# A hybrid decoder layer on one core: where ScalarE's two exponentials stand among its copies in the sparse attention

## The chip, the cores and the metric

The kernel runs on one NeuronCore of a Trainium2 chip. Its engines take their instructions in order, each from a queue of its own: TensorE (PE, with its weight loads as PEld), VectorE (DVE), ScalarE (ACT), GpSimd (POOL), and SyncE (SP), which here only issues transfers. They wait for each other through semaphores. The metric is the device time of one execution in microseconds (us).

## The reference, and what of it matters here

The layer is `LayerNorm(ALPHA * x + TokenMixer(x))` followed by `LayerNorm(ALPHA * x + MoE(x))` for 1024 tokens of width 1024. The token mixer projects x to 7308 columns and splits them among a convolution, a sliding window attention, a retention, and a native sparse attention. The last has three parts: attention over compressed keys, over chosen blocks of keys, and over a window of 512 keys:

```
kcmp = compress(kc, pe_k, w1_k, w2_k)
...
p_cmp = masked_softmax(sc, cdist >= 0)
...
_, sel = lax.top_k(imp, min(NSA_TOPN, nslc))
...
o_win = banded_attention(qh, kw[:, None], vw[:, None], slopes, NSA_WINDOW)
...
o = gt[0] * o_cmp + gt[1] * o_slc + gt[2] * o_win
```

The kernel computes the part over chosen blocks as attention over all keys up to the query, with a penalty on the blocks that were not chosen.

## The kernel before

The mixers are the first stage of the program, up to about 971 us; then come the merge of the four branches, the output projection, and the experts. In the mixers one list, `SCHEDULE`, written by `schedule()`, sets the order. Each engine's program walks through the whole list and issues its own share of each item. So an item that moves in the list moves on each engine that does something for it, and only there.

The projection is cut into quarters (`('mm', q)`: 12 matmuls on TensorE, L537). Two quarters make a half, which ScalarE copies out of its PSUM bank (L744 for the merge gates, with a store on its own queue, L746). The attention works on pairs of heads. The sparse attention has 32 pairs, numbered 16 to 47: for each block n of 128 queries (0 to 7) and each pair of heads c one of kind `win`, with min(n+1, 5) blocks of keys, and one of kind `sel`, with n+1 blocks. `attention(NSA, ...)` writes one step for each pair. A step holds, in this order:

- `score` of the coming pair k+1: matmuls on TensorE (L707) into banks that `max` of the pair before must have read;
- `max` of both heads of pair k+1: VectorE adds the distance term (L1021), reduces (L1024), and writes the negated maximum `m_neg` (L1029);
- `norm` of both heads of pair k on VectorE (L1040, L1041, L1047), after their exponentials; for a `sel` pair a table (L1003) goes ahead;
- for pair k-1 its probabilities in groups of two blocks of keys. For each group: `fill`, which is four transposes on TensorE into bank 6 (L544) and a copy of the bank to `w_t` on ScalarE (L835), both 128x512, or 128x256 where a last group has one block; then, where their turn has come, quarters of the projection; then `pv`, the product with the values (L729, for the first group of a `win` pair also L724) of the group before, on TensorE. A finished block of queries is copied to `out_t` by ScalarE (`out`, L843) behind the product that completes it, and GpSimd stores it (L508);
- `exp` of both heads of pair k+1 on ScalarE (L855, with a second, short instruction that reads the sum).

Bank 6 is a single buffer, so transposes of a group wait for the copy of the group before:

```
B = bank[6]
if f:
    pe.wait_ge(fill_out, f)
```

ScalarE's exponential waits for VectorE:

```
act.wait_ge(max_done, u + 1)
```

And the first product of a new block of queries waits for the copy of the last one but itself:

```
if first and c == 0 and t:
    pe.wait_ge(tile_out, t)
```

Of the kernel before, what the change touches and what calls it, by code (L numbers as in the profile page):

```python
# [162 lines left out]
def schedule():  # L163

    items = [('xt', g) for g in range(8)] + [('mm', 0), ('mm', 1)] + [('xt', g) for g in range(8, 16)]
    state = dict(q=2, fill=0, pv=0)
    last = 4 * NCH

    def adv(n):
        for _ in range(n):
            if state['q'] < last:
                items.append(('mm', state['q']))
                state['q'] += 1

    def upto(c):
        adv(max(0, 4 * c - state['q']))

    def fill(kind, *a):  # L180
        items.append(('fill', state['fill'], kind, a))
        state['fill'] += 1

    upto(WHERE['ret_q', 0])
    items.append(('conv_h',))
    for k in range(CONV_K):
        items.append(('tap', k))
        adv(2 if k % 3 == 0 else 1)
    adv(2)
    for c in ('conv_mean', 'conv_var', 'conv_out'):  # L190
        items.append((c,))
        adv(4)

    def retention(p):
        items.append(('ret_a', p, 0))
        for n in range(NT):
            adv(1)
            if n + 1 < NT:
                items.append(('ret_a', p, n + 1))
            items.append(('ret_b', p, n))  # L200
        items.append(('ret_norm', p))
        adv(11)
        for g in range(4):
            fill('ret', p, g)
        items.append(('ret_store', p))
    upto(WHERE['ret_g', (0, 1)] + 1)
    retention(0)
    upto(WHERE['ret_g', (1, 1)] + 1)
    retention(1)
    upto(WHERE['swa_v', 0] + 1)  # L210
    for g in range(2):
        fill('swa_v', g)
        adv(1)

    def attention(pairs, rate):

        debt = 0.0
        waiting = []

        def product():

            pr, blocks = waiting.pop()
            items.append(('pv', state['pv'], pr['p'], blocks))
            pr['last_pv'] = state['pv']
            state['pv'] += 1
            if pr['c'] == 1 and pr['kind'] != 'win' and blocks[-1] == pr['nb'] - 1:
                items.append(('out', pr['kind'], pr['n']))

        def both(what, k):  # L230
            for e in range(2):
                items.append((what, 2 * pairs[k]['p'] + e))
        for k in range(-1, len(pairs) + 1):
            if k + 1 < len(pairs):
                pr = pairs[k + 1]
                if pr['kind'] == 'sel' and pr['c'] == 0:
                    items.append(('sel_table', pr['n']))
                items.append(('score', pr['p']))
                both('max', k + 1)
            if 0 <= k < len(pairs):  # L240
                both('norm', k)
            if k < 1 and k + 1 < len(pairs):
                both('exp', k + 1)
            if k >= 1:
                prev = pairs[k - 1]
                groups = [tuple(range(a, min(a + 2, prev['nb']))) for a in range(0, prev['nb'], 2)]
                prev['first_fill'] = state['fill']
                prev['last_fill'] = state['fill'] + len(groups) - 1
                for g, blocks in enumerate(groups):
                    fill('pair', prev['p'], blocks, state['pv'] + len(waiting))  # L250
                    if g == 0 and k + 1 < len(pairs):
                        both('exp', k + 1)
                    debt += rate / len(groups)
                    adv(int(debt))
                    debt -= int(debt)
                    if waiting:
                        product()
                    waiting.append((prev, blocks))
        product()
    attention(SWA, 2.0)  # L260
    upto(WHERE['gate', 0] + 1)
    fill('gate')
    for g in range(2):
        fill('vsvw', g)
    fill('pe')
    adv(9)
    for l in range(0, CMP_LEN, HID_STEP):
        items.append(('hidden', l))
        adv(1)
    items.append(('hidden_t',))  # L270
    adv(1)
    items.append(('compress',))
    adv(1)
    for n in range(NT):
        items.append(('cmp_score', n))
        adv(3)
        fill('cmp', n)
    attention(NSA, (last - state['q']) / len(NSA))
    adv(last)
    return items  # L280
# [1770 lines left out]
```

## Time and profile before

| | before |
|---|---|
| median of 3 runs | 2333.38 us (2333.18 to 2339.36) |
| the profiled execution | 2330.48 us |
| its span in the profile | 2328.6 us |
| TensorE busy | 2149.6 us (92%) |
| VectorE busy | 967.4 us (42%) |
| ScalarE busy | 516.2 us (22%) |
| mean granted clock of TensorE | 0.963 |

The median is of three runs; the profile is of one more execution, whose time stands beside its span: 1.9 us lie outside the span. A row of waits says which engine and line stood idle, and which instruction of which engine ended it. In a timeline the idle time stands in brackets, just ahead of the row's instruction. The granted clock is a share of 2.4 GHz: 1.00 is 2.4 GHz, 0.50 is 1.2 GHz, and a value between is a stretch that had both.

### The profile page before, as it was taken

What the parts mean: (1) busy time and instruction counts of PE and PEld (TensorE: products, weight loads), DVE (VectorE), ACT (ScalarE), POOL (GpSimd) and SP (SyncE); (2) the same over time, 40 slices, a digit from 0 to 9 for tenths busy, and PEclk for the clock granted to TensorE, in tenths of its full rate; (3) what the DMA queues carried; (4) which work ended last, traced back from release to release, by engine and by line L of the source; (5) the groups of instructions that cost most, each with busy time, mean ns of one, the idle gap of its engine ahead of it and who ended that gap; (6) DMA issues with size and microseconds to landing.
All of it is one profiled execution on the core that took longest, in us unless ns stands there. A gap on an engine that the chain in (4) does not pass through costs nothing. (4 is left out here: it accounts for less than half of the span.)

```text
span 2328.6 us, 30293 instructions
## 1 busy us (share of the span) xinstructions
PE 2149.6 (92%) x9137; PEld 1349.2 (58%) x9138; DVE 967.4 (42%) x2281; ACT 516.2 (22%) x1049; POOL 509.5 (22%) x354
## 2 busy tenths in 40 slices
PE   7999999899999887689997979999999999999990
PEld 6887777677786655468454434555555555555540
DVE  2794615341266674378334402222223222222225
ACT  2111212341124443310111221222222111222212
POOL 2343232233221110012000322221212222222223
PEclk8999999999999998899998989999999999999995
DMA  5122120225121100277412166899898989978854
GB/s 170 52 68 91 60 64 28 84 55 138 61 85 60 42 26 16 77 238 245 156 63 109 45 264 190 292 343 333 277 328 272 305 280 338 330 246 293 288 152 162
DMA packets 162783, 391.62 MB, mean 168 GB/s; under 512 B 22257, under 2 KB 92178, under 8 KB 138001
## 3 DMA queue, kind: packets, MB, share of 16 engines
q1 hardware_dynamic: 126608, 292.78, 34.0%
q0 software_dynamic: 26880, 81.02, 15.6%
q10 hardware_dynamic: 9216, 16.78, 1.9%
q8 instruction: 49, 0.80, 0.1%
q14 instruction: 30, 0.24, 0.0%
HBM read 329.70 MB, written 75.50 MB: 174 GB/s over the span
## 5 line engine op out<-in xcount | busy, mean ns | idle before, releaser
L1642 PE MATMUL e_bank<-w_gu,work 128*128 x1216 | 554.7, 599 | 1.2 <-ACT work L1744 1.2
L537 PE MATMUL a_bank<-x_hi,w_hi 128*128 128x512 f32 x928 | 379.6, 409 | 8.6 <-DVE x_lo L897 8.6
L537 PE MATMUL a_bank<-x_lo,w_hi 128*128 128x512 f32 x928 | 368.2, 397 | 0.0
L537 PE MATMUL a_bank<-x_hi,w_lo 128*128 128x512 f32 x928 | 368.1, 397 | 0.0
L1642 PEld LDWEIGHTS e_bank<-w_gu,work 128*128 128x128 f32 x1216 | 220.2, 191 | 221.9 <-issue 221.6
L1656 PE MATMUL e_bank<-w_d,hid_t 128*128 x608 | 275.4, 596 | 1.1 <-ACT hid_t L1787 1.1
L1575 POOL DMA_INDIRECT acc<-work,idx_out x76 | 119.7, 1575 | 627.4 <-issue 607.4
L537 PEld LDWEIGHTS a_bank<-x_hi,w_hi 128*128 128x128 f32 x928 | 179.4, 193 | 50.8 <-issue 13.0
L537 PEld LDWEIGHTS a_bank<-x_hi,w_lo 128*128 128x128 f32 x928 | 178.4, 192 | 39.3
L537 PEld LDWEIGHTS a_bank<-x_lo,w_hi 128*128 128x128 f32 x928 | 178.8, 193 | 35.3 <-issue 0.5
L1656 PEld LDWEIGHTS e_bank<-w_d,hid_t 128*128 128x128 f32 x608 | 110.6, 192 | 111.9 <-issue 111.9
L480 POOL CAST w_hi<-w_raw 128x1024 fp32r<-128x1024 f32 x56 | 64.6, 1153 | 493.4 <-PE a_bank L537 493.4
L482 POOL TENSOR_TENSOR w_lo<-w_raw,w_hi 128x1024 fp32r<-128x1024 f32 x56 | 145.3, 2595 | 4.6
L1909 DVE TENSOR_TENSOR one_hot<-e_const,pos 128x1024 bf16 x78 | 95.6, 1226 | 110.8 <-issue 110.7
L1751 ACT ACTIVATE silu<-e_bank 128x256 f32<-128x256 f32 x76 | 29.2, 385 | 496.6 <-PE e_bank L1642 496.6
L1940 DVE SCALAR_TENSOR_TENSOR hidden<-e_bank,row_gate,silu 128x256 f32<-128x256 f32 x76 | 36.8, 484 | 239.0 <-ACT silu L1751 239.0
L1281 PE MATMUL e_bank<-work 128*128 128x512 f32 x256 | 111.4, 593 | 2.2 <-PEq L1104 2.2
L1631 PEld LDWEIGHTS e_bank<-e_const,work 128*128 128x128 f32 x608 | 79.5, 190 | 52.1 <-issue 35.1
L1536 POOL DMA_INDIRECT work<-x1d,idx x77 | 80.4, 1045 | 81.5 <-DVE idx L1927 48.2
L917 DVE SCALAR_TENSOR_TENSOR reg_b<-reg_b,conv_p 128x1024 f32<-128x1024 f32 x60 | 98.2, 1711 | 0.0
L1631 PE MATMUL e_bank<-e_const,work 128*128 128x128 f32 x608 | 80.7, 276 | 15.1 <-DMA work<-x1d,idx 12.6
L1744 ACT ACTIVATE work<-e_bank 128x512 f32<-128x512 f32 x152 | 82.5, 594 | 53.1 <-PE e_bank L1631 53.1
(322 smaller groups left out, 2416.3 us busy)
## 6 DMA issues: line engine op xcount, KB each, us to landing
w_gu<-in_moe_wg SPq DMA_DIRECT2D x64, 1024.0 KB
w_gu<-in_moe_wu SPq DMA_DIRECT2D x64, 1024.0 KB
w_d<-in_moe_wd SPq DMA_DIRECT2D x64, 1024.0 KB, 8.4
w_raw<-in_w_in SPq DMA_DIRECT2D x54, 512.0 KB, 3.6
gates<-gate_out ACTq DMA_DIRECT2D x64, 256.0 KB
g_sb<-gates SPq DMA_DIRECT2D x16, 1024.0 KB, 6.2
work<-in_w_out SPq DMA_DIRECT2D x4, 1024.0 KB, 8.8
late<-in_x SPq DMA_DIRECT2D x8, 512.0 KB, 3.6
```

What stands on the lines that cost most here:

```text
L480: pool.tensor_copy(w_hi[:, c % 2, :, :], w_raw[:, c % 2, :, :]).then_inc(w_hi_ready, 1)
L482: pool.tensor_tensor(w_lo[:, c % 2, :, :], w_raw[:, c % 2, :, :], w_hi[:, c % 2, :, :].bitcast(F32), ALU.subtract).then_inc(w_lo_ready, 1)
L537: ins = pe.matmul(bank[h][:, :], w[:, c % 2, k, :], x[:, k, cols], start=(k == 0 and j == 0), stop=(k == KD - 1 and j == 2))
L917: ins = dve.scalar_tensor_tensor(conv_y[:, c, :], conv_h[:, c, k:k + S], conv_p[:, c, k:k + 1], conv_y[:, c, :], ALU.mult, ALU.add)
L1281: ins = pe.matmul(bank[2 * (t % 2) + h][:, :], merged[:, k, t * P:(t + 1) * P], w_out[:, k, h * HALF:(h + 1) * HALF], start=k == 0, stop=k ...
L1536: pool.indirect_dma_start(out=x_g[:, s, :], out_offset=None, in_=x1d[:, :], in_offset=bass.IndirectOffsetOnAxis(ap=idx[:, s:s + 1], axis=0 ...
L1575: pool.indirect_dma_start(out=acc[:, :], out_offset=bass.IndirectOffsetOnAxis(ap=idx_out[:, s:s + 1], axis=0), in_=y_out[:, s, :], in_offs ...
L1631: ins = pe.transpose(bank[4 + k // 4][:, (k % 4) * P:(k % 4 + 1) * P], x_g[:, s, :].rearrange('p (c k) -> p k c', k=KD)[:, k, :], ident)
L1642: ins = pe.matmul(bank[s][:, :].rearrange('p (m f) -> p m f', m=2), x_gt[:, s, k, :], w_gu[:, bass.ds(e & 3, 1), :, k, :].rearrange('p a m ...
L1656: ins = pe.matmul(bank[2 + h][:, :], hid_t[:, j, :], w_d[:, bass.ds(e & 3, 1), j, h * HALF:(h + 1) * HALF].rearrange('p a f -> p (a f)'), ...
L1744: ins = act.activation(x_gt[:, s, 4 * h:4 * h + 4, :], bank[4 + h][:, :].rearrange('p (k c) -> p k c', k=4), ACT.Copy)
L1909: dve.tensor_tensor(one_hot[:, s, :, :], bcast(ranks, 1, NT), pos[:, :, bass.ds(e, 1)].broadcast_to([P, NT, P]), ALU.is_equal).then_inc(oh ...
```

## The change

The two `exp` items of the coming pair stood behind the `fill` of the step's first group (`g == 0`). Now they stand behind the `fill` of its last group. In a step with one group the two places are the same.

```
                 for g, blocks in enumerate(groups):
                     fill('pair', prev['p'], blocks, state['pv'] + len(waiting))
-                    if g == 0 and k + 1 < len(pairs):
+                    if g == len(groups) - 1 and k + 1 < len(pairs):
                         both('exp', k + 1)
                     debt += rate / len(groups)
                     adv(int(debt))
```

Only ScalarE does anything for `exp`. The order of its instructions is the only one that changes; those of TensorE, VectorE, GpSimd and SyncE stand as before. The sliding window attention, whose pairs have at most two blocks of keys and so one group, has no step that changes.

The first place is ScalarE's share of the step that scores pair 45 (the chosen blocks of n = 7, first two heads) and transposes pair 43 (seven blocks, four groups). `reg_a<-a_bank` are the copies of transposed groups, `gate_out` is a half of the projection, and the two 128x1024 are the exponentials. Before:

```order
L855 ACTIVATE reg_s,den<-reg_s,m_neg 128x1024 x2
L835 ACTIVATE reg_a<-a_bank 128x512 x2
L835 ACTIVATE reg_a<-a_bank 128x256
L835 ACTIVATE reg_a<-a_bank 128x512
L855 ACTIVATE reg_s,den<-reg_s,m_neg 128x640 x2
```

The row ahead of these is the copy of the step's first group, 128x512; the last two rows are the next step's first copy and its exponentials. After:

```order
L835 ACTIVATE reg_a<-a_bank 128x512 x3
L835 ACTIVATE reg_a<-a_bank 128x256
L855 ACTIVATE reg_s,den<-reg_s,m_neg 128x1024 x2
L835 ACTIVATE reg_a<-a_bank 128x512
L843 ACTIVATE out_t<-a_bank 128x256
```

The second, third and fourth copy of pair 43 went ahead of the exponentials of pair 45, and the next step's first copy follows them at once.

The second place is the step behind it, which scores pair 46 (window, n = 7) and transposes pair 44 (five blocks, three groups). Before, from its exponentials on:

```order
L855 ACTIVATE reg_s,den<-reg_s,m_neg 128x640 x2
L843 ACTIVATE out_t<-a_bank 128x256
L835 ACTIVATE reg_a<-a_bank 128x512
L744 ACTIVATE gate_out<-a_bank 128x512
L746 DMA gates<-gate_out 128x512
L835 ACTIVATE reg_a<-a_bank 128x256
```

And after, from the copy of its first group on:

```order
L835 ACTIVATE reg_a<-a_bank 128x512
L843 ACTIVATE out_t<-a_bank 128x256
L835 ACTIVATE reg_a<-a_bank 128x512
L744 ACTIVATE gate_out<-a_bank 128x512
L746 DMA gates<-gate_out 128x512
L835 ACTIVATE reg_a<-a_bank 128x256
L855 ACTIVATE reg_s,den<-reg_s,m_neg 128x640 x2
```

Here the copy to `out_t`, two copies of groups, and the copy of a half with its store went ahead of the exponentials.

## Rows read from the trace of the kernel before

**Rows 1.** The page: busy times of the engines, and the chain that ended last.

```profile
PE 2149.6 (92%) x9137; PEld 1349.2 (58%) x9138; DVE 967.4 (42%) x2281; ACT 516.2 (22%) x1049; POOL 509.5 (22%) x354
...
PE 38%; DMA 1%; DVE 1%; issue 1%; POOLq 0%; POOL 0%; SPq 0%; ACT 0%; ACTq 0%
```

**Rows 2.** Waits, 720 to 966 us: who for whom, sum, times, longest.

```profile
DVE reg_s L1021 <- PE a_bank L707: 77.8, 23, 8.3
...
ACT reg_s L855 <- DVE m_neg L1029: 34.2, 42, 1.6
...
PE a_bank L544 <- ACT reg_a L835: 23.3, 19, 4.8
...
PE a_bank L724 <- ACT out_t L843: 8.8, 5, 3.3
...
PE a_bank L544 <- DVE reg_s L1047: 0.7, 1, 0.7
```

**Rows 3.** Busy time of each engine, 720 to 965 us; then clock, DMA share, GB/s.

```profile
720.00:965.00 245.00, 211.78 (x1351) 143.53 (x1350) 145.45 (x361) 94.24 (x199) 29.50 (x21) 0.94 0.10 33
```

**Rows 4.** Timeline of GpSimd's and SyncE's queue, where the mixers end.

```profile
971.30 0.71 POOL L508 DMA_DIRECT2D yt<-out_t  x1 [32.12 <-ACT out_t L843]
...
977.49 0.37 SPq L1128 DMA_DIRECT2D p_raw<-in_p_conv  x1
```

**Rows 5.** Timeline of TensorE: start, us, instruction, in brackets the idle time ahead.

```profile
805.12 0.44 PE L724 MATMUL a_bank<-reg_a,v_cmp 63*64 63x128 f32 x4 [3.26 <-ACT out_t L843]
...
865.81 0.66 PE L544 MATMUL a_bank<-a_const,reg_s 128*128 128x128 f32 x4
...
869.53 0.66 PE L544 MATMUL a_bank<-a_const,reg_s 128*128 128x128 f32 x4
...
873.66 0.66 PE L544 MATMUL a_bank<-a_const,reg_s 128*128 128x128 f32 x4 [2.89 <-ACT reg_a L835]
...
917.54 0.66 PE L544 MATMUL a_bank<-a_const,reg_s 128*128 128x128 f32 x4
...
918.88 0.66 PE L544 MATMUL a_bank<-a_const,reg_s 128*128 128x128 f32 x4 [0.32 <-ACT reg_a L835]
...
924.90 1.12 PE L544 MATMUL a_bank<-a_const,reg_s 128*128 128x128 f32 x4 [4.78 <-ACT reg_a L835]
...
931.64 1.35 PE L707 MATMUL a_bank<-reg_b 64*128 64x512 f32 x8
```

**Rows 6.** Timeline of ScalarE in the step that scores pair 45.

```profile
918.23 0.60 ACT L835 ACTIVATE reg_a<-a_bank 128x512 f32<-128x512 f32 x1 [2.48 <-PE a_bank L544]
...
921.53 0.19 ACT L855 ACTIVATION_READ_ACCUMULATOR reg_s<-reg_s,m_neg 128x1 f32 x1
923.13 1.15 ACT L855 ACTIVATE reg_s<-reg_s,m_neg 128x1024 f32<-128x1024 f32 x1 [1.41 <-DVE m_neg L1029]
924.28 0.57 ACT L835 ACTIVATE reg_a<-a_bank 128x512 f32<-128x512 f32 x1
```

**Rows 7.** Timeline of VectorE in the same step.

```profile
922.94 0.15 DVE L1029 TENSOR_SCALAR m_neg<-m_raw 128x1 f32<-128x1 f32 x1
...
924.30 0.61 DVE L1047 TENSOR_SCALAR reg_a<-reg_a,rden,gate_n 128x640 f32<-128x640 f32 x1
```

**Rows 8.** Stretches behind long waits, and one without: columns as in rows 3.

```profile
805.00:810.00 5.00, 4.88 (x24) 3.86 (x25) 0.56 (x1) 0.84 (x2) 0.71 (x1) 0.66 0.08 30
870.00:895.00 25.00, 18.74 (x103) 12.75 (x102) 8.33 (x23) 6.99 (x14) 3.09 (x3) 0.80 0.07 26
900.00:905.00 5.00, 3.71 (x18) 2.76 (x19) 1.33 (x4) 2.22 (x5) 0.00 (x0) 0.66 0.00 0
925.00:930.00 5.00, 5.00 (x16) 3.93 (x16) 0.00 (x0) 0.60 (x1) 0.00 (x0) 0.61 0.00 0
950.00:955.00 5.00, 5.00 (x33) 3.58 (x32) 1.48 (x4) 1.79 (x3) 0.00 (x0) 0.72 0.00 0
810.00:825.00 15.00, 11.56 (x83) 7.62 (x82) 7.14 (x19) 4.50 (x9) 3.39 (x2) 1.00 0.05 17
```

More of the change, by code:

```diff
@@ L250, in attention @@
                     fill('pair', prev['p'], blocks, state['pv'] + len(waiting))
-                    if g == 0 and k + 1 < len(pairs):
+                    if g == len(groups) - 1 and k + 1 < len(pairs):
                         both('exp', k + 1)
```

## The prediction, made before the changed kernel was run

> **What bounds the kernel now.** I read the page first: TensorE is busy for 92% of the span and every other engine for 42% or less, and the chain that ended last is TensorE's work as far as it reaches, 38% of the span out of the 41% that it names [rows 1]. All of that lies in the experts and says nothing yet of the mixers. So the second view is that of the waits in the stretch where the sparse attention runs, 720 to 966 us. The busy times show TensorE at 211.8 of 245 us, VectorE at 145.5 and ScalarE at 94.2 [rows 3], which leaves TensorE 33.2 us idle. The waits say where: 23.3 us in 19 waits of the transposes (L544) for ScalarE's copy of the group before (L835), 8.8 us in 5 waits of a first product (L724) for the copy to `out_t`, 0.7 us for VectorE [rows 2]. That is 32.8 us, so TensorE is idle here for these three reasons and no others, and two of the three are ScalarE. The end of this stretch goes straight on: the last `out_t` copy releases the store at 971.30, and the merge's first load is issued at 977.49 [rows 4]. A TensorE that is done earlier moves all that follows.
>
> Third, the timeline, for what stands in front of those copies. Of the 19 waits, 12 are of 0.32 us, as the one at 918.88 [rows 5]: transposes, copy, transposes through one bank, a cycle of 1.34 us (917.54 to 918.88), in which the product leaves 0.32 us uncovered. The other seven are together 23.3 - 12 x 0.32 = 19.5 us, with 2.89 at 873.66 and the longest, 4.78, at 924.90. That one is typical. ScalarE copied the step's first group at 918.23, then waited for VectorE's maxima and ran both exponentials, the second at 923.13, and only at 924.28 copied the second group, whose transposes had started at 918.88 [rows 5, 6]. ScalarE stood idle within those exponentials for want of the maxima: 34.2 us of such waits in the stretch [rows 2]. It is not short of time, it stands in the wrong wait.
>
> **What the change does, term by term.** It adds and removes no instruction. In 22 steps (those that transpose pairs 24 to 45: from pair 24 on a pair has two groups or more, and with pairs 46 and 47 no exponential is left) the copies of all groups go ahead of both exponentials. The halves of the projection, with their stores on ScalarE's queue, and `out_t` move ahead with them. No transfer on SyncE's or GpSimd's queue is moved past another.
>
> Term A, the seven long waits: the copy that TensorE waits for has no exponential ahead of it in its step any more. What is left is the cycle, 0.32 us each: 19.5 - 7 x 0.32 = 17.2 us.
>
> Term B, `out_t`: 8.8 us in five waits, the longest that of 3.26 at 805.12 [rows 2, 5]. The copy now waits only for the product and for one group's copy, while TensorE transposes the next group (0.66 us). I leave 0.1 us each: 8.3 us. From both sides: nothing left gives 8.8, and 0.32 each gives 7.2.
>
> Term C, the clock. Behind long waits the granted clock fell: 0.66, 0.80, 0.66, 0.61 and 0.72 in five stretches of 5, 25, 5, 5 and 5 us, and rows 5 have a wait of 3.26, 2.89 and 4.78 us at the head of the first, in the second and at the head of the fourth. That is, TensorE ran for part of them at 1.2 instead of 2.4 GHz. The stretch from 810 to 825, where TensorE was idle for 15 - 11.56 = 3.4 us in all, kept 1.00 [rows 8]. At 1.2 GHz the same matmuls take twice as long, so a stretch loses its length times one less the clock: 1.7 + 5.0 + 1.7 + 1.95 + 1.4 = 11.8 us. If all long waits go, the clock has nothing left to fall on, and all of it comes back. If it does not follow the waits, nothing does. I take 11.8, since what is left resembles the stretch at 1.00, and keep 0 for the range.
>
> By the Trainium skill, TensorE: Matmul & The Clock Gate, section Why this matters for your kernels, idle gaps between bursts of matmuls return the array to half rate; that agrees with rows 8 and with term C. The same page, section A second HAM failure mode: psum-queue depth-cycling, says that frequent very short idle times between groups of matmuls, as a bank is cycled, can do it too. By that rule the waits of 0.32 us, of which the change leaves more, would hold the clock where it is, term C would be 0, and the sum 11.8 us smaller; it has its place among the rivals.
>
> Term D, what the exponentials are in front of now: the next step's first copy, and behind it the next transposes. I work it out where they are longest, the step that scores pair 45. Transposes: first group 917.54, second 918.88, third 1.34 us on, 920.22; a quarter stands behind the third, and a cycle with a quarter takes 3.72 us (865.81 to 869.53), so the fourth 923.94. Its copy begins 0.69 us behind its transposes (917.54 to 918.23) and ends by 925.2. The exponentials' maxima are there at 923.1 [rows 7], so both run without a wait, 1.15 us each with the reading of the sum (923.13 to 924.28) [rows 6], to 927.5. TensorE meanwhile ends the cycle, at most 1.34 us, and scores pair 46 in 1.35 [rows 5]: the next first group at 926.6 at the latest, its copy could begin at 927.3. The exponentials hold it for 0.2 us, or for 0.6 if the fourth group, with one block of keys, ends its cycle 0.4 us sooner. This is so for the three steps that transpose pairs of seven or eight blocks and score another; in the others the exponentials are shorter with the keys, and where a quarter stands behind the last group it covers them. I take 3 x 0.6 = 1.8 us of new waits.
>
> Term E, VectorE. It normalises pair k after the maxima of k+1, and in the example the exponentials end at 927.5, when it has only begun the maxima of pair 46 behind its score, 926.6. So it does not wait for them. What could become late is VectorE itself, as steps get shorter. In the example its last maximum is done at 923.1, its last normalisation at 924.9, and TensorE's next score comes at about 925, the transposes of pair 44 that need that normalisation at 926.6 [rows 5, 7]. So it holds, by 1.7 us at its longest pair. Over the stretch VectorE is busy for 145.5 us, and idle for 77.8 us for the scores alone [rows 2, 3]. I take 0; a wait of 0.5 us in each of the 22 steps, 11 us, is the other end.
>
> At the end nothing is scored any more, and the last normalisation follows the last exponentials at once: copy 0.69 + 0.60, exponentials 2 x 1.15, two normalisations some 2 us (922.94 to 924.91) [rows 6, 7], 5.6 us. Three groups of pair 46 with a quarter, 2 x 1.34 + 3.72 = 6.4 us, stand on TensorE before pair 47 is wanted, and cover it: nothing.
>
> Sum: 17.2 + 8.3 + 11.8 - 1.8 = 35.5 us. Against the profiled execution's own time, 2330.48 us (1.9 us of it outside the span), that gives 2295.0; the median of the runs shown is 2.9 us above that execution, so 2333.38 - 35.5 = 2297.9, and I say 2298.
>
> **The rivals.**
>
> The clock does not come back (with it the page's rule on short idle times): the waits go, rows 8 stay. For it: the remaining waits are many, one for nearly every group. Against it: 810 to 825 at 1.00 with the same short waits in it. Price: 35.5 - 11.8 = 23.7 us, time 2310. Chance 0.15.
>
> The waits move: with TensorE's steps shorter, the transposes wait for VectorE's normalisation, or for copies behind exponentials more often than in term D. For it: VectorE's 1.7 us of room in the example, and its operations can be slower while GpSimd splits weights. Against it: nearly every step carries a quarter of 2.4 us or more. Price: term E's 11 us and half of term C, 17 us, time 2315. Chance 0.12.
>
> Slower: the exponentials, now in front of the next step's first copy, are fully exposed there. Two of them take 2.3 us where they are longest; in 22 steps that is at most 51 us against 17.2 + 8.3 + 11.8 = 37.3 of gain, 13 us slower, 2347. It decides at 37.3 / 22 = 1.7 us a step; my rows give 0.6 in three of them. Chance 0.05.
>
> No change: the waits are only where another limit shows, and VectorE or the maxima take all of them over; TensorE's total idle time stays at 33 us. Against it: VectorE's 77.8 us of idle time. Chance 0.05, time within 7 us of 2333.
>
> **How the numbers follow.** The forecast, 2290 to 2305, has 0.63. Its own bounds: all 33.2 us of idle time and 11.8 of clock gone would be 45 us, 2288. The range reaches down to that and up over the clock's rival and nearly to that of moved waits: 2288 to 2315, some 0.83. A measurement of this kernel tells a change from none at about 0.3%, 7 us. Faster: 0.63 + 0.15 + 0.12 = 0.90; same 0.05; slower 0.05.
>
> **What would show it.** Between 720 and the end of the sparse attention the waits of L544 for L835 should number 20 or more, none over 1.2 us, 7 to 9 us together; those of L724 for `out_t` under 1 us together (A, B). The granted clock should be 1.00 there (C). The exponentials (L855) should wait for `m_neg` for under 10 us instead of 34.2, and the last `out_t` store should be issued at about 936 instead of 971.30. What follows it should take as long as before. A wait of L544 for L1047 in many steps, or of L707 for `m_neg`, would show the moved waits; a clock under 1.00 with no long wait ahead of it, the clock's rival; and a stretch that is shorter while the end is not, a limit behind the mixers that I have not seen.

## The result and the profile after

The changed kernel takes 2295.91 us (median of 4 runs, 2293.35 to 2301.93), the kernel before 2336.37 us in the same runs. The ratio is 0.983, with a 95% interval from 0.9804 to 0.9857: 40 us less, or 33 to 46 us by the interval. Two single runs further down (2364.32 us, of the kernel behind the second group, and 2355.73 us, of that with the doubled maximum) were in a slower state, at a lower clock than the others of their kernel, and are left out of its median. The profiled execution took 2295.86 us with a span of 2294.0, 34.6 us less than the span before.

The page, engines and chain, against [rows 1]:

```profile
PE 2139.6 (93%) x9137; PEld 1342.1 (59%) x9138; DVE 968.3 (42%) x2281; ACT 514.3 (22%) x1049; POOL 510.2 (22%) x354
...
PE 17%; DMA 11%; issue 10%; DVE 2%; DVEq 1%; POOLq 0%; POOL 0%; ACT 0%; ACTq 0%
```

The work is the same; TensorE's busy time is 10 us less because the same matmuls ran at a higher clock in the mixers, as the stage below shows. The chain again covers the experts only, and says nothing of the mixers; what it follows there differs from one execution to the next (TensorE's share of it is 17% here and 23% in a second profile of the same kernel).

Where the mixers end, against [rows 4]:

```profile
934.64 0.71 POOL L508 DMA_DIRECT2D yt<-out_t  x1 [31.98 <-ACT out_t L843]
...
940.84 0.37 SPq L1128 DMA_DIRECT2D p_raw<-in_p_conv  x1
```

The last store of `out_t` is issued 36.7 us sooner than at 971.30. From there to the end of the span it takes 1359.4 us, before 1357.3. In the eleven profiles that follow, of kernels that change nothing behind the mixers, this remainder lies between 1357 and 1372 us, so it varies by itself. The time ahead varies too: the executions reach the first maximum of pair 26, whose exponentials are the first that the change moves, up to 3.5 us apart. So I read fine differences from a stretch with two fixed ends, "the stage": from that maximum to this store. The maxima before and after:

```profile
745.51 0.15 DVE L1029 TENSOR_SCALAR m_neg<-m_raw 128x1 f32<-128x1 f32 x1
745.30 0.15 DVE L1029 TENSOR_SCALAR m_neg<-m_raw 128x1 f32<-128x1 f32 x1
```

And the busy times and the clock in the stage, before and after:

```profile
745.51:971.30 225.79, 191.70 (x1236) 130.04 (x1236) 128.26 (x305) 85.73 (x177) 21.73 (x17) 0.94 0.08 28
745.30:934.64 189.34, 180.92 (x1236) 122.28 (x1236) 127.50 (x305) 83.91 (x176) 21.88 (x16) 1.00 0.10 34
```

The stage is 36.4 us shorter: TensorE is idle for 8.4 us instead of 34.1, which is 25.7 us, and busy for 10.8 us less with the same 1236 matmuls, which is the clock.

The waits from 720 to 931 us, a stretch that begins and ends a little ahead of the stage, against [rows 2] (who for whom, sum, times, longest), and the busy times of the same stretch, against [rows 3]:

```profile
DVE reg_s L1021 <- PE a_bank L707: 43.8, 21, 3.7
...
PE a_bank L544 <- ACT reg_a L835: 4.4, 14, 0.4
ACT reg_s L855 <- DVE m_neg L1029: 2.6, 7, 0.5
...
PE a_bank L724 <- ACT out_t L843: 0.7, 1, 0.7
PE a_bank L544 <- DVE reg_s L1047: 0.7, 1, 0.7
PE a_bank L544 <- DVE reg_a L1047: 0.7, 1, 0.7
```

```profile
720.00:931.00 211.00, 203.25 (x1368) 137.42 (x1367) 145.25 (x360) 93.23 (x201) 29.47 (x21) 1.00 0.11 38
```

TensorE's wait for ScalarE's copies fell from 23.3 to 4.4 us and for `out_t` from 8.8 to 0.7. Its idle time is 211 - 203.25 = 7.75 us against 33.2, and the granted clock is 1.00 throughout instead of 0.94. VectorE does the same 145 us of work in 34 us less; its waits for the scores take the difference.

The step that scores pair 45, against [rows 5 to 7]. TensorE, with the quarter's matmuls between the third group (893.85) and its product left out:

```profile
891.17 0.66 PE L544 MATMUL a_bank<-a_const,reg_s 128*128 128x128 f32 x4
891.75 0.44 PE L729 MATMUL a_bank<-reg_a,reg_b 128*64 128x128 f32 x4
892.51 0.65 PE L544 MATMUL a_bank<-a_const,reg_s 128*128 128x128 f32 x4 [0.32 <-ACT reg_a L835]
893.09 0.66 PE L729 MATMUL a_bank<-reg_a,reg_b 128*64 128x128 f32 x8
893.85 0.66 PE L544 MATMUL a_bank<-a_const,reg_s 128*128 128x128 f32 x4
...
898.73 1.35 PE L707 MATMUL a_bank<-reg_b 64*128 64x512 f32 x8
...
901.43 0.33 PE L544 MATMUL a_bank<-a_const,reg_s 128*128 128x128 f32 x1 [0.40 <-ACT reg_a L835]
```

ScalarE, whose last copy of the step is the one at 898.25, and VectorE's second maximum:

```profile
898.25 0.38 ACT L835 ACTIVATE reg_a<-a_bank 128x256 f32<-128x256 f32 x1 [3.10 <-PE a_bank L544]
898.53 1.14 ACT L855 ACTIVATE reg_s<-reg_s,m_neg 128x1024 f32<-128x1024 f32 x1
899.57 0.19 ACT L855 ACTIVATION_READ_ACCUMULATOR reg_s<-reg_s,m_neg 128x1 f32 x1
899.66 1.14 ACT L855 ACTIVATE reg_s<-reg_s,m_neg 128x1024 f32<-128x1024 f32 x1
900.70 0.19 ACT L855 ACTIVATION_READ_ACCUMULATOR reg_s<-reg_s,m_neg 128x1 f32 x1
900.79 0.58 ACT L835 ACTIVATE reg_a<-a_bank 128x512 f32<-128x512 f32 x1
```

```profile
896.57 0.15 DVE L1029 TENSOR_SCALAR m_neg<-m_raw 128x1 f32<-128x1 f32 x1
```

The third group's transposes come 1.34 us behind the second's, where 4.78 us of idle time stood. The second maximum is there at 896.7, 1.8 us before ScalarE starts even the first exponential, so the two run back to back. The next step's first copy follows them at 900.79; its transposes began at 900.01 and a copy begins 0.69 us behind them, so without the exponentials it would have come at 900.70. They hold it for 0.1 us.

### The profile page after: what moved, and what is told of

The parts are those of the page before. It is cut to its first block and busy times, and to the rows that moved or that the text cites. A ratio compares the mean times of both kernels' runs of the same rounds, so it can differ in the third digit from the quotient of the medians.

```text
span 2294.0 us, 30293 instructions
## 1 busy us (share of the span) xinstructions
PE 2139.6 (93%) x9137; PEld 1342.1 (59%) x9138; DVE 968.3 (42%) x2281; ACT 514.3 (22%) x1049; POOL 510.2 (22%) x354
```

## The experiments

All ratios are against the kernel before in the same runs. "End" is the start of the last `out_t` store in the profile, "stage" the stretch from the first maximum of pair 26 to it.

| kernel | median us | ratio to before (95%) | end us | stage us |
|---|---|---|---|---|
| before | 2336.37 | | 971.3 | 225.8 |
| changed, as in the result | 2295.91 | 0.983 (0.9804 to 0.9857) | 934.6 | 189.3 |
| changed, once more | 2299.68 | 0.984 (0.9813 to 0.9868) | 935.1 | 189.3 |
| behind the first product | 2331.51 | 0.9964 (0.9947 to 0.9981) | 967.2 | 221.4 |
| behind the second group | 2305.2 | 0.9854 (0.9823 to 0.9885) | 939.1 | 195.0 |
| at the step's end | 2300.91 | 0.9832 (0.9805 to 0.986) | 936.6 | 189.9 |
| old place, one step late | 2302.91 | 0.9867 (0.9841 to 0.9892) | 938.6 | 194.7 |
| before, work in the waits | 2325.12 | 0.9939 (0.9916 to 0.9961) | 958.9 | 215.7 |
| before, short maximum | 2318.7 | 0.9925 (0.9896 to 0.9953) | 953.7 | 209.0 |
| changed, short maximum | 2296.16 | 0.9828 (0.9803 to 0.9853) | 932.7 | 188.2 |
| only steps of two groups | 2339.93 | 1.0015 (0.9995 to 1.0035) | 974.2 | 229.2 |
| changed, two steps back | 2307.2 | 0.987 (0.9844 to 0.9895) | 945.6 | 201.4 |
| changed, maximum taken twice | 2307.27 | 0.988 (0.9849 to 0.9912) | 946.9 | see there |

The two profiles of the changed kernel give the same stage to 0.01 us, where their ends differ by 0.45. The stage is still one execution of each kernel, and that of the kernel before, with its falls of the clock, was profiled only once. The medians tell kernels apart by about 6 us at best, and differ from the stage by up to 8 us in what they put between two kernels; I cannot say why.

### Is `out_t` a loss of its own?

```
                     if waiting:
                         product()
+                    if g == 0 and k + 1 < len(pairs):
+                        both('exp', k + 1)
                     waiting.append((prev, blocks))
```

(The two lines behind `fill` are taken out.)

> Both exponentials stand behind the product that follows the first group, not behind the first group's transposes: the halves of that place and the copy to out_t go ahead of them, the copies of the second and later groups do not. If the out_t waits (term B) were a loss of their own beside the waits of the transposes, this alone would give back 8.3 us and the clock that fell behind the two of 3.3 us, 1.7 + 3.2 us: 13 us faster than before. My theory now is that both are one wait: with out_t ahead TensorE runs on to the third group's transposes, and there waits for the second copy, still behind the exponentials, some 3 us. Then 0 to 3 us faster than before; few waits of L724 for L843, but those of L544 for L835 grow from 23 to about 30 us.

Waits from 720 to 962 us:

```profile
PE a_bank L544 <- ACT reg_a L835: 27.5, 21, 4.8
...
PE a_bank L724 <- ACT out_t L843: 0.7, 1, 0.7
```

The waits of L724 are gone (8.8 to 0.7 us), and those of the transposes grew from 23.3 to 27.5. The stage is 4.4 us shorter, more than the 0 to 3 that I gave it, and far from 13. So terms A and B are largely one wait: what is let past at `out_t` is caught at the next copy, and 4 us of it is all that this part gives alone.

### Which copies must go ahead?

```
-                    if g == 0 and k + 1 < len(pairs):
+                    if g == min(1, len(groups) - 1) and k + 1 < len(pairs):
```

> The exponentials stand behind the second group's copy (behind the only one where there is one): steps with one or two groups are as in the changed kernel, steps with three or four have only the first two copies ahead. Theory (the wait for the maxima is what costs, and the second copy comes late enough to cover most of it): steps of three groups lose nothing, since the third copy is wanted only in the next step; the three steps with four groups that score another pair wait 2 to 3 us for the third copy. 5 to 9 us slower than the changed kernel, 28 to 34 us faster than before. Rival (every copy behind an exponential stalls the next transposes): half of the gain or less, under 20 us faster than before.

The stage is 5.6 us longer than in the changed kernel. The longest wait on TensorE's timeline is the fourth group of the step that scores pair 43:

```profile
879.19 0.33 PE L544 MATMUL a_bank<-a_const,reg_s 128*128 128x128 f32 x1 [2.73 <-ACT reg_a L835]
```

In the other two steps with four groups a quarter stands ahead of the fourth, and the longest waits are 0.69 and 0.78 us. Idle time makes 3.9 us of the 5.6, the clock the rest: it fell once, behind this wait. So 85% of the gain needs only the second copy ahead. The size is in the 5 to 9 us that I expected, though one step waited and not three; the rival is out.

Only steps with exactly two groups moved:

```
-                    if g == 0 and k + 1 < len(pairs):
+                    if g == (len(groups) - 1 if len(groups) == 2 else 0) and k + 1 < len(pairs):
```

> Only steps with exactly two groups (pairs 24 to 31, and the window pairs of n = 2 and 3) have the exponentials behind the last group; steps with three or four groups stay as before. Theory: in the short steps a quarter stands between the groups and hides the exponentials, only one out_t wait of 1.27 us is there: 0 to 2 us faster than before, not to be told from it. Rival (the gain is spread over all 22 steps): 8/22 of 37 us, 13 us faster.

No gain: the sum of TensorE's waits for the copies is 23.3 us in 19, the same to the tenth as before. The stage is 3.5 us longer than before, where I expected it to be up to 2 us shorter. TensorE's idle time in it is 0.5 us less, its busy time 4.0 us more: the clock was lower (0.92 from 720 to 969 us, before 0.94):

```profile
720.00:969.00 249.00, 216.23 (x1358) 146.44 (x1358) 144.87 (x359) 93.72 (x198) 29.51 (x21) 0.92 0.10 32
```

The difference lies behind two waits, 2.5 us and 1.5 us by the clock. Behind the waits of 2.80 us (818.00 before, 816.91 here) and 2.21 us (855.22 and 856.70) the clock stayed at 1.00 in the kernel before and fell here; before, then here:

```profile
818.00:823.00 5.00, 5.00 (x31) 3.46 (x31) 0.33 (x1) 0.98 (x2) 1.59 (x2) 1.00 0.04 17
855.00:860.00 5.00, 4.78 (x32) 3.52 (x33) 3.40 (x9) 1.61 (x4) 0.07 (x1) 1.00 0.13 50
817.00:822.00 5.00, 5.00 (x13) 4.04 (x14) 0.23 (x1) 0.38 (x1) 0.00 (x0) 0.50 0.00 0
857.00:862.00 5.00, 5.00 (x28) 3.34 (x27) 1.96 (x5) 1.20 (x2) 0.00 (x0) 0.70 0.03 11
```

So the gain lies in steps of three and four groups, and the same waits do not always cost the same clock.

### How much room is there behind the last group?

```
                     if waiting:
                         product()
+                    if g == len(groups) - 1 and k + 1 < len(pairs):
+                        both('exp', k + 1)
                     waiting.append((prev, blocks))
```

(The two lines behind `fill` are taken out.)

> The exponentials stand at the very end of the step, behind the last group's product and the halves there. Theory: where a half is finished behind the last group, ScalarE first waits for it and copies it, so the exponentials start some 3.5 us later and hold the next step's first copy by 1 to 1.5 us, in about five steps: 2 to 7 us slower than the changed kernel, 28 to 36 us faster than before, with some waits of L544 of about 1 us. Rival (there is room behind the last group for anything, as VectorE wants the exponentials only behind the next maxima): no difference from the changed kernel.

The stage is 0.6 us longer than in the changed kernel, less than the 2 to 7 us of the theory: the rival, no difference, came true. TensorE's waits for copies are 5.1 us in 15, the longest 0.6. The theory had 1 to 1.5 us in each of five steps; in the timeline three waits, of 0.39, 0.60 and 0.39 us, are longer than the usual 0.32. The room is larger than I worked out.

### The wait for the maxima, or the exponentials' own run time?

First the old place, with exponentials whose maxima are long there:

```
-                    if g == 0 and k + 1 < len(pairs):
-                        both('exp', k + 1)
+                    if pairs is SWA:
+                        if g == 0 and k + 1 < len(pairs):
+                            both('exp', k + 1)
+                    elif g == 0 and 2 <= k < len(pairs):
+                        both('exp', k)
```

> The exponentials stand again behind a step's first group, but they are those of pair k, whose maxima were taken a whole step ago, not those of k+1. They still run in front of the second copy, but wait for nothing. Theory: their own run time of 1.9 to 2.3 us holds the second copy by 1 to 1.5 us wherever no quarter stands between, in some 10 of the steps with three or four groups; no wait over 2.9 us, so the clock stays at 1.00: 8 to 18 us slower than the changed kernel, 20 to 30 us faster than before. Rival (run time and waiting cost alike): 10 us faster than before or less.

The stage is 5.4 us longer than in the changed kernel and 31.1 us shorter than before, a little outside both ranges: the run time costs two thirds of the least that I gave it. The clock from 720 to 934 us is 1.00. The longest of TensorE's waits and two of the three of 0.86 us (this kernel's lines stand three lower):

```profile
869.78 0.44 PE L727 MATMUL a_bank<-reg_a,v_cmp 63*64 63x128 f32 x4 [1.75 <-ACT out_t L846]
879.62 0.33 PE L547 MATMUL a_bank<-a_const,reg_s 128*128 128x128 f32 x1 [0.86 <-ACT reg_a L838]
...
897.90 0.66 PE L547 MATMUL a_bank<-a_const,reg_s 128*128 128x128 f32 x4 [0.86 <-ACT reg_a L838]
```

The two of 0.86 us are in the steps where 4.08 and 4.78 us stood before. So the exponentials can run in front of the second copy at little cost: all but 5 us of the loss came from their waiting there for VectorE.

Then the waiting made shorter, before and after the change:

```
-                    order.after(dve.reduce_max(m_raw[:, s:s + 1], soft[s][:, 0:L], AX.X))
+                    order.after(dve.reduce_max(m_raw[:, s:s + 1], soft[s][:, (0 if kind == 'swa' else L - P):L], AX.X))
```

> The kernel before, where VectorE reduces the maximum of a pair of the sparse attention over its last 128 columns only (the query's own block; the softmax is the same for any shift, so what is left out is the exact maximum, and in bits the result differs). The reductions take about 0.28 us instead of 0.82 (640 columns) or 1.22 (1024), so the second exponential can start 1.1 to 1.9 us sooner. Theory (what costs in the place before is mostly that ScalarE waits there for VectorE's maxima): each of the nine long waits shrinks by that, some 12 us, and as few stay above 2.9 us most of the clock comes back: 15 to 24 us faster than before. Rival (what costs is the exponentials' own run time in front of the copies): 0 to 4 us faster.

> The same shorter maximum in the changed kernel. Theory: ScalarE no longer waits for the maxima (3 us left) and TensorE hardly for VectorE (1.4 us left), so VectorE's time saved buys nothing: within 2 us of the changed kernel. Rival (VectorE had become the next limit): 4 us faster or more.

In the kernel before, the stage is 16.8 us shorter. From 720 to 948 us:

```profile
PE a_bank L544 <- ACT reg_a L835: 13.1, 17, 2.9
ACT reg_s L855 <- DVE m_neg L1029: 12.8, 33, 1.2
PE a_bank L724 <- ACT out_t L843: 5.1, 3, 2.2
```

TensorE's two waits are 13.9 us shorter (32.1 to 18.2), and the clock of the stretch is 0.96.
```profile
815.00:820.00 5.00, 4.45 (x14) 3.55 (x14) 0.80 (x3) 0.88 (x3) 0.00 (x0) 0.66 0.00 0
```

In the changed kernel the same edit makes the stage 1.1 us shorter, and the median, 2296.16, stays where the changed kernel's are. VectorE's maxima set the length of the old waits; behind the change next to nothing hangs on them.

### Does the clock belong to the waits?

The kernel before, with matmuls whose result nobody reads just ahead of eight of its long waits: an item `busy` ahead of the third group's `fill` in the steps that score pairs 35, 39, 41, 43, 45 and 47, and ahead of the first product in those of 34 and 42. `q` is the next quarter; the bank is the one of the two projection banks that has been copied out:

```
+                elif what == 'busy':
+                    q, n = item[1:]
+                    h, t = q // 2 % 2, q // 2
+                    B = bank[h] if q % 2 == 0 else bank[1 - h]
+                    pe.wait_ge(half_out, t - 1 if q % 2 == 0 else t)
+                    for i in range(n):
+                        pe.matmul(B[:, :], x_hi[:, 0, 0:P], x_hi[:, 0, 0:HALF], start=True, stop=True)
```

> The kernel before, with 79 matmuls of 128x512 added whose results nobody reads, 6 to 16 at each of eight places where TensorE stood in a long wait (six before a third group's transposes, two before a first product), sized to about 0.7 of the wait. At 0.23 us each they are 18 us of TensorE's time at full clock. Theory (term C: the clock falls because of the long idle times, and that costs 11.8 us beside the waits): they fit into the waits, the clock stays at 1.00 in the sparse attention, and the kernel is 7 to 12 us faster than before though it does more. Rival (the clock is not tied to the waits, or term C was counted twice): 0 to 10 us slower than before, with the clock of the stretch at 0.94 as before.

The stage is 10.1 us shorter, within the 7 to 12 us of the theory, though TensorE does 79 matmuls more. Waits and busy times from 720 to 953 us (the lines stand up to 13 lower):

```profile
PE a_bank L550 <- ACT reg_a L848: 8.6, 19, 0.9
...
PE a_bank L737 <- ACT out_t L856: 4.3, 5, 1.3
```

```profile
720.00:953.00 233.00, 218.78 (x1417) 149.00 (x1417) 143.21 (x356) 93.19 (x197) 28.12 (x20) 1.00 0.10 34
```

No wait is longer than 1.3 us and the clock is 1.00. ScalarE waits for the maxima as long as before (33.7 and 8.0 us), so the stalls themselves are all still there, filled with work. In the stage:

```profile
743.14:958.86 215.72, 200.63 (x1315) 136.55 (x1315) 127.46 (x305) 85.75 (x176) 22.02 (x17) 1.00 0.09 30
```

At the same clock of 1.00 TensorE is busy for 19.7 us more than in the changed kernel (200.63 against 180.92): that is what the added work takes, and it fills 19.0 us of idle time (34.1 before, 15.1 here). What came back is the clock alone, and it is the same 10.8 us as in the changed kernel: term C, apart from A and B.

### One step at a time

The old place in the two steps with the longest waits, in an otherwise changed kernel:

```
+                    late = pairs is SWA or k + 1 not in (27, 29)
-                    if g == len(groups) - 1 and k + 1 < len(pairs):
+                    if g == (len(groups) - 1 if late else 0) and k + 1 < len(pairs):
```

> The changed kernel, with the exponentials back behind the first group in two steps only, those that score pairs 43 and 45, where the kernel before had its two longest waits, 4.08 and 4.78 us. Theory (each step's wait and the fall of the clock behind it are that step's own): both waits come back, 8.9 us less the two cycles of 0.32, and behind each the clock falls for some 4 us, 1.7 to 2 us each: the stage ends 11 to 13 us later than in the changed kernel. Rival (the waits in many steps add to each other, or later steps catch up): 5 us or less, or over 18 us.

The stage is 12.1 us longer than in the changed kernel, within the 11 to 13 us that I expected. The two waits are back to the hundredth:

```profile
879.14 0.47 PE L545 MATMUL a_bank<-a_const,reg_s 128*128 128x128 f32 x1 [4.08 <-ACT reg_a L836]
...
902.96 1.12 PE L545 MATMUL a_bank<-a_const,reg_s 128*128 128x128 f32 x4 [4.78 <-ACT reg_a L836]
```

TensorE is idle for 8.5 us more and busy for 3.6 us more, which is the clock behind them, 1.8 us each where I expected 1.7 to 2. The stretches behind the two waits:

```profile
879.00:889.00 10.00, 9.54 (x55) 6.76 (x56) 1.98 (x5) 1.66 (x4) 0.00 (x0) 0.79 0.00 0
903.00:913.00 10.00, 9.68 (x55) 7.00 (x56) 1.81 (x5) 1.85 (x4) 0.14 (x1) 0.80 0.00 0
```

The size of the waits is that of the same steps in the kernel before, whatever the other steps do: each step's wait is its own.

### How far is VectorE from being the limit?

```
                     order.after(dve.reduce_max(m_raw[:, s:s + 1], soft[s][:, 0:L], AX.X))
+                    if kind != 'swa':
+                        order.after(dve.reduce_max(m_raw[:, s:s + 1], soft[s][:, 0:L], AX.X))
```

> The changed kernel, in which VectorE takes each maximum of the sparse attention twice, so its work grows by 1.6 to 2.4 us in a step with five to eight blocks and less in shorter ones, some 43 us in all; the result is the same. Theory (VectorE has little room in the longest steps, 1.7 us by my account, and much in the others): TensorE's next score or its transposes begin to wait for VectorE in some of the steps, 3 to 12 us slower than the changed kernel. Rival (VectorE, busy for 145 of 211 us, has room everywhere): within 2 us of it. Other rival (VectorE is as good as the bound already): 25 us slower or more.

This edit lengthens steps ahead of pair 26 too, so here the stretch begins at the first distance term of the sparse attention (L1021, at 694.40, in the changed kernel at 697.93). It is 15.8 us longer than in the changed kernel (252.5 against 236.7), past the upper edge of 12; the median is 8 us longer (2307.3 against 2299.7 in the same runs), within it. From 720 to 931 us:

```profile
PE a_bank L544 <- DVE reg_s L1049: 6.7, 5, 2.1
...
PE a_bank L544 <- DVE reg_a L1049: 4.3, 4, 2.5
PE a_bank L707 <- DVE m_neg L1031: 0.8, 2, 0.5
```

With 42 us more work VectorE is late for the normalisations in nine places, 11 us together. In the stretch TensorE is idle for 11.3 us more and busy for 4.5 us more, which is the clock. The wait that would come next if steps got shorter still is this one. But the theory placed it wrongly: five of the nine, with 7.1 of the 11 us, come before 800 us, in steps that transpose pairs of at most four blocks, where I saw much room.

The changed kernel once more:

> The changed kernel unedited, beside the two others on one chip, for an interval of its own: 35 to 40 us faster than before, its mixers at an end 36 to 37 us sooner.

Its end is at 935.09, 36.2 us sooner than before, its stage is as long as in the first profile, and its waits are the same; the median is 38 us under that of before.

## Why the prediction was right

I forecast 2298 us within 2288 to 2315; it is 2295.91, and 2299.68 in the later runs. Against the profiled execution the sum said 35.5 us, and the span fell by 34.6: 36.7 up to the stage's end, less 2.1 of the remainder's own variation. The stage alone is 36.4 us shorter. The medians fell by 40.5 and 38.5 us; the 2 to 4 us above the stage lie within the interval, and I do not know where they come from. Part of the closeness is luck: terms A, B and D together came out 2.0 us too small, and term C 1.0 us too large. By its steps:

**Terms A and B, less D.** They came to 17.2 + 8.3 - 1.8 = 23.7 us of idle time; measured 34.1 - 8.4 = 25.7 in the stage. The sum held, two parts of it less well. A and B are not two losses, as the kernel with `out_t` alone ahead shows: it gave 4 us, not 8.3. Adding them was right only because the change removes both. And I left a cycle's 0.32 us where each long wait went; there are 14 waits of 4.4 us in all, not the "20 or more, 7 to 9 us" that I named. The timeline after shows why: the 0.32 us stand at 892.51, behind a product of one block (four matmuls, 0.44 us), and not at 893.85, behind one of two blocks (eight, 0.66 us), which covers the copy. The seven long waits stood behind products of two blocks for the most part and left nothing.

**Term D**, 1.8 us, was mis-sized: 0.1 us in the example, and nothing elsewhere, as of the 14 waits that are left thirteen are 0.32 us or less and one is 0.40. I had 0.2 and 0.6 for a step and took the upper. The kernel with the exponentials at the step's end says the same: even there they cost 0.6 us.

**Term C**, 11.8 us. The clock is 1.00 in the whole stretch, and the same matmuls keep TensorE busy for 10.8 us less. The rows put a little too much on it: the stretch from 870 to 895 us counts 6.3 us of idle time as if a low clock cost something in it. The kernel with work in its waits gives the same 10.8 us back with ScalarE's waits unchanged, so the fall came from the idle time and not from anything else that the change touches. The Trainium skill's rule in TensorE: Matmul & The Clock Gate, Why this matters for your kernels, agrees: idle gaps between bursts lower the clock. Its section A second HAM failure mode: psum-queue depth-cycling, by which short idle times could do the same and term C would have been nothing, did not show at this size: 14 waits of 0.3 to 0.4 us in 211 us, and those of up to 1.3 us in the filled kernel, left the clock at 1.00.

**Term E**, nothing. TensorE waits 1.4 us for normalisations, 0.7 of them new. Twice the maximum overruns VectorE's room, but mostly in the short steps, so the 1.7 us that I worked out for the longest was not the least.

**The rivals.** The clock came back; the waits did not move to VectorE; the exponentials' place in front of the next first copy never cost what would turn the sign. My reading of the cause, that ScalarE "stands in the wrong wait", is shown from two sides: with the maxima long there, the old place costs 5.4 us; with shorter maxima it costs 16.8 us less. The 34.2 us of waits that I named for it left out 8.0 us more, of the exponentials whose scores stand in `reg_a`; no term used either number.

## What to carry to other kernels

An engine at 22% can hold the one at 92% if it waits in order in front of something small that the other needs: look at what stands ahead of the late instruction and ask what that one was waiting for, not how long it runs. Place the instruction that waits behind the copies that release others, as long as its own reader comes later; here the three places tried between the second copy and the step's end gave 85% of the gain or more. Where TensorE is the bound, price its long idle times twice, once as idle time and once as the clock behind them, which was here another 11 us on 26, and see in the trace that the clock fell there.

## What the runs showed of the hardware that was not expected

Work that nobody needs made a kernel faster. 79 matmuls of 128x512, 19.7 us of TensorE's time at full clock, put into idle times of 2 to 5 us, made the stage 10.1 us shorter, as the matmuls behind them ran at 2.4 instead of 1.2 GHz.

The same waits did not cost the same clock in each profile. With 23.3 and 8.3 us of them in the kernel with two-group steps moved, the stretch had 0.92, with 23.3 and 8.8 in the kernel before 0.94; behind a wait of 2.80 us the clock was 0.50 for 5 us in the one and 1.00 in the other. Nor does the length of a single wait decide it: with the short maximum a wait of 1.73 us had 0.66 behind it, and one of 2.20 us, which ends at 877.92, had 1.00 (the row below). So the bound of 2.9 us that my expectations used does not hold. What decides it these runs do not show, nor whether it is the program or the execution: each of these kernels was profiled once, and the mean clock of the kernel before lies between 0.957 and 0.964 over its runs here.

```profile
878.00:883.00 5.00, 5.00 (x36) 3.60 (x38) 0.63 (x1) 1.24 (x3) 1.50 (x2) 1.00 0.06 26
```
